# Attentions carried as side work of a projection and of two gated merges

## The reference, cut to what matters

```python
h = rms_norm(x, norm1_g)
proj = h @ w_in
y_a = mlstm_branch(...)          # ends in a norm over each head, times a gate
y_b = gqa_branch(...)            # 8 heads of 64 on 2 key heads, softmax over 512 keys
y_c = natten_branch(...)         # 8 heads of 64, windows of the 8 x 64 grid, with a bias
y_d = diff_branch(...)           # 4 heads, softmax(q1 k1) - lam * softmax(q2 k2), then a norm
g = sigmoid(gl).reshape(bsz, s, 4, D_MODEL)
merged = (g[:, :, 0] * (y_a @ w_up_a) + g[:, :, 1] * (y_b @ w_up_b)
          + g[:, :, 2] * (y_c @ w_up_c) + g[:, :, 3] * (y_d @ w_up_d))
x = x + merged @ w_out
h2 = rms_norm(x, norm2_g)
x = x + (silu(h2 @ w_ffn_gate) * (h2 @ w_ffn_up)) @ w_ffn_down
```

## Time and profile before

| what | value |
|---|---|
| median of 3 runs | 3935.73 us (3926.63 to 3938.5) |
| the profiled execution, time | 3938.49 us |
| its span from first to last instruction | 3936.6 us |
| PE busy | 3687.2 us, 94% |
| DVE, ACT, POOL busy | 2034.0 (52%), 1537.6 (39%), 399.3 (10%) us |
| mean granted PE clock, as a share of 2.4 GHz | 0.966 |

### The profile page before, as it was taken

How to read it: one execution, slowest core, us unless ns; L and a number is a source line. 1 busy time by engine, 2 the same in 40 slices (tenths; PEclk the granted TensorE clock), 3 DMA queues, 4 the chain that set the end, 5 groups by cost and what they waited for, 6 DMA issues and landing times. The chain is left out here.

```text
span 3936.6 us, 52179 instructions
## 1 busy us (share of the span) xinstructions
PE 3687.2 (94%) x20468; PEld 2879.9 (73%) x20468; DVE 2034.0 (52%) x3128; ACT 1537.6 (39%) x2410; POOL 399.3 (10%) x353
## 2 busy tenths in 40 slices
PE   7898989969999999999899999999899899999998
PEld 5456777758878887676667878887676667888887
DVE  4879565585443334646556443333546646454332
ACT  4464332543342233435453333323334444233322
POOL 0018233000011110310000001100010000001100
PEclk9899889979999999999999999999999999999999
DMA  3011001203332332120212332233111212332232
GB/s 110 22 41 59 7 2 61 70 11 117 91 100 98 97 95 85 43 70 28 97 48 88 96 100 96 96 95 92 55 59 38 82 48 81 96 102 96 96 92 80
DMA packets 83487, 289.31 MB, mean 73 GB/s; under 512 B 9168, under 2 KB 9296, under 8 KB 82000
## 3 DMA queue, kind: packets, MB, share of 16 engines
q1 hardware_dynamic: 83136, 286.30, 22.9%
q10 hardware_dynamic: 144, 0.15, 0.0%
HBM read 284.32 MB, written 2.10 MB: 73 GB/s over the span
## 5 line engine op out<-in xcount | busy, mean ns | idle before, releaser
L484 DVE TENSOR_TENSOR weights_lo_r<-raw_weights,weights_hi_r 128x1024 fp32r<-128x1024 f32 (+2 forms) x554 | 636.9, 1150 | 1457.7 <-ACT weights_hi_r L478 1457.3
L478 ACT ACTIVATE weights_hi_r<-raw_weights 128x1024 fp32r<-128x1024 f32 (+2 forms) x554 | 547.5, 988 | 1610.9 <-PE ps L553 1556.2
L552 PE MATMUL ps<-xn_r,weights_hi_r 128*128 128x512 f32 x2688 | 1056.1, 393 | 0.0
L551 PE MATMUL ps<-xn_hi,weights_hi_r 128*128 128x512 f32 x1632 | 670.1, 411 | 40.8 <-DVE weights_lo_r L484 12.1
L553 PE MATMUL ps<-xn_hi,weights_lo_r 128*128 128x512 f32 x1632 | 644.7, 395 | 0.0
L552 PEld LDWEIGHTS ps<-xn_r,weights_hi_r 128*128 128x128 f32 x2688 | 510.3, 190 | 112.8 <-issue 11.0
L551 PE MATMUL ps<-y_r,weights_hi_r 128*128 128x512 f32 x1200 | 471.8, 393 | 8.0 <-DVE weights_lo_r L484 5.9
L553 PE MATMUL ps<-y_r,weights_lo_r 128*128 128x512 f32 x1200 | 468.5, 390 | 0.0
L551 PEld LDWEIGHTS ps<-xn_hi,weights_hi_r 128*128 128x128 f32 x1632 | 312.1, 191 | 137.5 <-issue 56.8
L553 PEld LDWEIGHTS ps<-xn_hi,weights_lo_r 128*128 128x128 f32 x1632 | 311.9, 191 | 67.5
L551 PEld LDWEIGHTS ps<-y_r,weights_hi_r 128*128 128x128 f32 x1200 | 226.5, 189 | 60.3 <-issue 11.9
(11 more groups left out here) (547 smaller groups left out, 5271.5 us busy)
## 6 DMA issues: line engine op xcount, KB each, us to landing
raw_weights<-in_w_ffn_dram SPq DMA_DIRECT2D x132, 512.0 KB, 3.7
raw_weights<-in_w_down_dram SPq DMA_DIRECT2D x48, 512.0 KB, 3.5
raw_weights<-in_w_out_dram SPq DMA_DIRECT2D x24, 512.0 KB, 3.6
bias_table<-in_window_bias_dram SPq DMA_DIRECT2D x8, 1280.0 KB, 9.8
raw_weights<-in_w_down_dram SPq DMA_DIRECT2D x24, 384.0 KB, 3.1
raw_weights<-in_w_hgrn_dram SPq DMA_DIRECT2D x16, 512.0 KB, 3.5
raw_weights<-in_w_mix_ssm_dram SPq DMA_DIRECT2D x16, 512.0 KB, 3.8
raw_weights<-in_w_a_qk_dram SPq DMA_DIRECT2D x16, 512.0 KB, 3.4
```

The source lines that it names most:

```text
L478: act.activation(self.k.w_hi[:, g % 2, 0:chunk.width], self.k.raw[:, slot, 0:chunk.width], ACT.Copy)\
L484: dve.tensor_tensor(self.k.w_lo[:, g % 2, 0:chunk.width], self.k.raw[:, slot, 0:chunk.width], self.k.w_hi[:, g % 2, 0:chunk.width].bitcast ...
L551: pe.matmul(out, w_hi, x_hi, start=start, stop=False)
L552: pe.matmul(out, w_hi, x_lo, start=False, stop=False)
```

## The change

- Three attentions no longer have a stage of their own. diff runs beside the projection c (`project_beside`), gqa and after it the transposition of c's values beside a merge a (`gated_beside` with `InTurn`), window beside a merge b. The merges c and d stay in `gated_products`. The order of the merges is now a, b, c, d.
- Projection and merges beside an attention use banks 0 and 1 only, and the scores have banks 2 and 3 alone. S of step n therefore waits for the readers of step n-1, not n-2.
- In an attention piece PE does S, PV, T. A piece comes at the middle of each 24-matmul chunk as well as at the end of every chunk: 24 places in each of the three stages. gqa, diff and window have 19 pieces each on PE (16 steps and 3 to drain).
- `norm_a` runs beside the projection b, which has 6 chunks.
- The gates of these layers are made as tanh of half the logit, plus 1, times the value; the factor 1/2 goes into the split of `mixed`. The multiplication becomes a `scalar_tensor_tensor` of one instruction as before.
- The bias table of the window attention is three buffers of one pair of heads instead of one of four pairs. The fourth pair is loaded by ACT's queue.

```diff
+def project_beside(k, outputs, src, side):
...
+                for s in range(job.body):
+                    t, g = job.t0 + s, job.g0 + s
+                    if t >= 2:
+                        pe.wait_ge(tile_used, t - 1)
+                    pe.wait_ge(stream.parts_ready, g + 1)
+                    for q in range(kt):
...
+                        mm = three_passes(pe, bank(k.ps, t % 2), k.w_hi[:, g % 2, at], k.w_lo[:, g % 2, at],
+                                          src.hi[:, q, :], src.lo[:, q, :], q == 0, q == kt - 1)
+                        if q == kt // 2 - 1:
+                            next(pieces, None)
+                    mm.then_inc(stream.chunk_used, 1)
+                    next(pieces, None)
...
+def gated_beside(k, part, dst, gate, side):
...
+            for t in range(KD):
+                next(pieces, None)
+                act.wait_ge(stream.chunk_used, job.g0 + 2 * t + 1)
+                if t:
+                    act.wait_ge(summed if part.accumulate else value_taken, t)
+                open_gate(act, gate, bank(k.ps, 0), part.func).then_inc(gate_ready, 1)
+                stream.run_ahead(stream.make_hi, act, job, 0, True, 2 * t, AHEAD_PARTS)
+                next(pieces, None)
+                stream.run_ahead(stream.make_hi, act, job, 0, True, 2 * t + 1, AHEAD_PARTS)
+                next(pieces, None)
...
@@ class Attention, tensor @@
-                if n >= 2:
+                if n:
                     if self.bias_of is None:
-                        pe.wait_ge(self.exps, 2 * (n - 1))
+                        pe.wait_ge(self.exps, 2 * n)
                     else:
-                        pe.wait_ge(self.fronts, self.front * (n - 1))
+                        pe.wait_ge(self.fronts, self.front * n)
                 for s in range(2):
-                    mm = pe.matmul(bank(k.ps, 2 * (n % 2) + s), self.q_of(2 * g + s, c)[:, i * P:(i + 1) * P],
+                    mm = pe.matmul(bank(k.ps, 2 + s), self.q_of(2 * g + s, c)[:, i * P:(i + 1) * P],
...
@@ layer_branches @@
+            norm_a = HeadNorm(y_a, A_HEADS, P, f"a_norm{n}", k.const("eps")[:, 0:1], o_gate, centre=True)
+            project(k, [(f"w_b_q{n}", b_qk[:, 0:4, :], 1.0), (f"w_b_k{n}", b_qk[:, 4:5, :], 1.0),
+                        (f"w_b_v{n}", v, 1.0)], k.xn, beside=norm_a)
...
+        project_beside(k, [(f"w_c_v{n}", y_c, 1.0), (f"w_c_q{n}", c_qk[:, 0:4, :], 0.125),
+                           (f"w_c_k{n}", c_qk[:, 4:8, :], 1.0)], k.xn, diff_attention(y_d, d_qk, d_v, lam, slope))
...
+            merge_beside(k, f"w_mix_a{n}", y_a, lo_a, mixed, False, InTurn(gqa, setup))
...
+            merge_beside(k, f"w_mix_b{n}", y_b, lo_b, mixed, True, window_side)
```

More of the change, by code:

```diff
@@ L1049, in project, with open_gate, gate_product @@
         return LastTile(jobs[0].dst, *leaves, end) if leaves else None
+def open_gate(act, o, src, func):
+    return act.activation(o, src, func, scale=0.5 if func is ACT.Tanh else 1.0)
+def gate_product(dve, o, gate, value, func):
+    if func is ACT.Tanh:
+        return dve.scalar_tensor_tensor(out=o, in0=gate, scalar=1.0, in1=value, op0=ALU.add, op1=ALU.mult)
+    return dve.tensor_tensor(o, gate, value, ALU.mult)
 class Gated:
@@ new lines, with __init__, open, sync @@
+class InTurn:
+    def __init__(self, first, second):
+        self.first, self.second = first, second
+    def open(self, k, ctx):
+        self.first.open(k, ctx)
+        self.second.open(k, ctx)
+    def sync(self, sp):
+        self.first.sync(sp)
+        self.second.sync(sp)
+    def tensor(self, pe):
+        yield from self.first.tensor(pe)
+        yield from self.second.tensor(pe)
+    def scalar(self, act):
+        yield from self.first.scalar(act)
+        yield from self.second.scalar(act)
+    def vector(self, dve):
+        yield from self.first.vector(dve)
+        yield from self.second.vector(dve)
+    def gpsimd(self, pool):
+        yield from self.first.gpsimd(pool)
+        yield from self.second.gpsimd(pool)
@@ L3525, in tensor @@
                 mm.then_inc(self.pv_done, 1)
+            m = self.done(n - 2)
+            if m is not None:
+                pe.wait_ge(self.norms, self.norm * (m + 1))
+                if m:
+                    pe.wait_ge(self.taken, m)
+                for s in range(2):
+                    for j in range(NT):
+                        mm = pe.transpose(k.ps[:, 4 + s, j * P:(j + 1) * P],
+                                          self.exp[:, maps * m % self.RE, s, j * P:(j + 1) * P], k.const("ident"))
+                mm.then_inc(self.turned, 1)
             yield
@@ L3723, in scalar @@
     def scalar(self, act):
-        yield
         for m in range(4):
@@ L3759, in bias @@
         at = window_at(b) + s * w * P
-        return self.table[:, g, at:at + w * P]
+        return self.pairs[g % 3][:, at:at + w * P]
     def tensor(self, pe):
@@ L3796, in tensor @@
                 mm.then_inc(self.pv_done, 1)
+            m = n - 2
+            if 0 <= m < self.N:
+                g, b, lo, w = self.place(m)
+                pe.wait_ge(self.norms, 3 * (m + 1))
+                if m:
+                    pe.wait_ge(self.taken, m)
+                for s in range(2):
+                    for j in range(w):
+                        mm = pe.transpose(k.ps[:, 4 + s, j * P:(j + 1) * P],
+                                          self.exp[:, m % self.RE, s, j * P:(j + 1) * P], k.const("ident"))
+                mm.then_inc(self.turned, 1)
             yield
@@ L3934, in merge @@
             parts = Parts(src, lo, y_hi[:, at:at + src.shape[1], :])
-            at += src.shape[1]
-            gated.append(Gated(w, k.xn, parts, ACT.Sigmoid, bool(gated), Split(parts), 1, beside))
-        parts = Parts(mixed[:, :, :], mixed_lo[:, :, :], y_hi[:, 0:KD, :])
+            at += KD if begun else src.shape[1]
+            gated.append(Gated(w, k.xn, parts, func, bool(gated or begun), Split(parts), 1, beside))
+        parts = Parts(mixed[:, :, :], mixed_lo[:, :, :], y_hi[:, 0:KD, :], 0.5 if func is ACT.Tanh else 1.0)
         remaining = gated_products(k, gated, mixed, gate, parts)
@@ L3940, in merge, with merge_beside @@
         return project(k, [(w_out, k.x, "add")], parts, remaining, beside=Together(*sides), leaves=sides)
+def merge_beside(k, name, y, y_lo, mixed, accumulate, side):
+    with ExitStack() as ctx:
+        k.line_start(ctx)
+        y_hi = ctx.enter_context(k.nc.sbuf_tensor(f"y_hi_{k.nc.next_id()}", [P, 4, T], F32R))
+        gate = k.sbuf(ctx, "gate", [P, 1, T])
+        parts = Parts(y, y_lo, y_hi[:, :, :])
+        part = Gated(name, k.xn, parts, ACT.Tanh, accumulate, Split(parts), 1)
+        gated_beside(k, part, mixed, gate[:, 0, :], side)
 class ScaledEnd:
@@ L4166, in hybrid_program @@
+            pairs = k.sbuf(inner, "pair_bias", [P, 2, pair])
+            window_side = WindowAttention(n, y_c, c_qk, c_v, [first_pair[:, 0, :], pairs[:, 0, :], pairs[:, 1, :]])
+            merge_beside(k, f"w_mix_b{n}", y_b, lo_b, mixed, True, window_side)
+        window.close()
+        return merge(k, [(f"w_mix_c{n}", y_c, lo_c, norm_d), (f"w_mix_d{n}", y_d, lo_d, None)], f"w_out{n}",
+                     f"norm2_{n}", y_lo[:, 8:16, :], y[:, 3:6, :], ACT.Tanh, (mixed, mixed_lo))
 def hybrid_program(nc, dram, const_at, n_const, col_at, n_col):
```

308 lines of the change are left out of this document (206 added, 102 removed).

## The result

The changed kernel took 3907.71 us (median of 3, 3905.23 to 3907.77), the kernel before 3935.73 (3926.63 to 3938.5): ratio 0.9938 with a 95% interval of 0.9922 to 0.9954, 0.6% faster. The forecast was 3907. The profiled execution has a span of 3905.5 us against 3936.6.

A forecast was written before the change was run, and what follows sets the result against it. PE was taken as the bound, busy 94% of the span. Stages summed to 609.2 us a layer against 620.9 and 625.65, 28.1 gained: 3910.4 profiled, 3907 us median, range 3882 to 3934.

The forecast's parts named there:

- c with diff: Diff beside projection c: 66.3 us of projection plus 41.0 of attention, 107.3 against 126.2, gain 18.9.
- PE has the same matmuls to do, so only its pauses can be won: gqa, diff and window stages: together they hold about 27 us of PE idle time in a layer.
- The tail of `norm_a`: 10 us idle: End of projection b: PE idles 10 us behind DVE's last tiles, the stage taking 49.8 instead of 33.85 us.
- The clock behind the tail: Projection d: half clock after the new, longer pause adds 3.4 us, 88.7 becoming 92.1.
- S on one pair of banks waits for nothing: S in attention pieces: wait taken as 0, with 0.2 to 0.3 us to spare in gqa.
- The sign that I had named for the contrary: Rows of S waiting for ACT exponentials or DVE statistics: more than some 5 us a layer means waits or slower.
- The other sign: L555 behind T: a distance of 0.11 to 0.2 us, else a drain at every border.
- Second layer: Second layer's stretch: the same 609.2 us against 625.65, 16.4 gained, its extra 4.7 us put down to lower clock.
- The larger gain: Rival at `norm_a`'s tail: it holds PE less or the clock does not fall; gain 55 us, 3880; chance 0.12.
- The waits: Rival at S: gqa's reserve gone and DVE late in diff, 0.2 us at each of 96 S, 3926; chance 0.12.
- The slower case: Rival at S on single banks: late ACT or DVE stops the merge too; 3965 at 0.6 us each; chance 0.10.
- A drain at every border: Rival between projection and attention: full drain of 0.16 us at each of 114 pieces, 18 us, 3925; chance 0.06.

The follow-up runs named there:

- e4: Changed kernel with diff in a stage of its own, on two pairs of score banks, then projection c alone; 3936.66 us, ratio 1.0023 to before.
- e5: Changed kernel with gqa in a stage of its own, in its old form on two pairs of score banks; 3917.00 us, ratio 0.9961 to before.
- e1: Changed kernel with `norm_a` tighter, its pieces beside projection b moved earlier; 3882.35 us, ratio 0.9881 to before.
- e10: Changed kernel with 9 unused fp32 matmuls of constants on PE behind `norm_a`'s last one; 3900.93 us, ratio 0.9918 to before.
- e3: Changed kernel with the two layers' gates by sigmoid and a plain product instead of tanh; 3916.75 us, ratio 0.9965 to before.
- e6: Changed kernel with gqa in a stage of its own, in its new form on one pair of score banks; 4049.93 us, ratio 1.0306 to before.

## Why the prediction was right

The time, the sum and its terms held. First layer, predicted and measured: projection b 49.8 and 49.9, projection d 92.1 and 90.6, c with diff 107.3 and 109.8, merge a 120.2 and 120.5, merge b 102.7 and 103.3, merges c and d 137.1 and 137.2; in all 609.2 and 611.3.

That both layers together came out within 0.3 us (1218.4 and 1218.1) is in part luck. Projection d came out 5.7 us shorter than predicted in the two layers (184.2 and 178.5), c with diff 3.4 longer (214.6 and 218.0), the other stages 2.0 longer together. The prediction counted nothing outside the layers, where 2.7 us went by chance of the clock. And 3935.73 - 28.1 is 3907.6, where the forecast says 3907.

- *PE has the same matmuls to do, so only its pauses can be won.* Right. By part and for both layers: diff about 29 us (e4), gqa 10 (e5), window some 6 (39.46 + 66.8 - 103.3, twice; no run of its own). The `norm_a` beside projection b takes back about 18: 49.9 for 33.85 us, less the 7.0 of matmuls that leave the merges, twice. 29 + 10 + 6 - 18 = 27, of 28.4 measured; two profiles of the kernel before differ by as much (1246.6 and 1248.1).
- *The tail of `norm_a`: 10 us idle.* Right, to 0.2 us, and by its own mechanism: e1 takes VectorE's tiles forward and 8.7 us of the stage go; e10 fills PE and the stage stays.
- *The clock behind the tail.* I added 3.4 us to projection d; against before it grew by 1.9 in the first layer and by nothing in the second (88.7 and 89.0 before, 90.6 and 87.8 after). Against e10, where the pause is filled, it is 3.6 and 1.3 longer. Most of the first stretch at half clock lies in the pause itself, and in the second layer none follows the wait for `lambda`. This term was mis-sized: 6.8 us for both layers, where e10 gives 4.9.
- *c with diff* came out 2.5 us longer in the first layer, 0.9 in the second. The first layer's clock was 0.98, after a pause at the end of projection d. The rest is 0.9, at full clock (108.2 us in e1). Of it, 0.2 lies in the projection itself (66.5 alone in e4 for 66.3). Read from start to start in e1's trace, S, T and PV hold PE 38.0 us, where the prediction had 41.0, and the fp32r matmuls around them 70.3, where they take 66.5 alone. So the borders move time from the attention to the matmuls that follow a piece or precede S, and cost 0.7 to 0.8 us net, which the prediction took as 0.
- *S on one pair of banks waits for nothing.* Right; the 0.2 to 0.3 us of reserve is 0.23 by e3. The sign that I had named for the contrary, more than 5 us in the row of S waiting for the exponentials, was a bad one: 5.3 us stand there without any lost time. The starts decide, not the sum of a wait. The other sign, L555 behind T at 0.11 to 0.2 us and else a drain at every border, was bad too: L555 starts 0.03 us after the last matmul of T starts, so by its letter the sign spoke for a drain, while the distance is shorter than the range and not longer.
- *Second layer.* I took 609.2 and said that the 4.7 us more of before were clock. The second run of before (625.25 and 622.9) shows that the layers trade such stretches by chance.

The rivals. The larger gain (3880 without tail and clock loss) did not come with the change, but it was about the right price of the tail: it meant 55 us less than before, and e1, which takes the tail away, has layers 52.5 us shorter and a median 47 shorter than the kernel before in its group. The waits did not come. The slower case needed 0.3 us for each S; e6 shows PE waiting for ACT at fifteen S in the bare stage, some 2.5 us each, and that the merge's matmuls hide such waits. A drain at every border was priced at 0.16 us; the traces show 0.18 for a change behind T and 0.09 more at the entry into S (0.32 for 0.23 us). Its count was wrong: with T last, gqa and window have three changes of tile a step and diff has two, as before. The Trainium skill, TensorEngine Tiling (Array Packing), section Key Properties, says that changing the tiling mode drains the engine; the trace agrees in that a change of tile costs time, 0.18 us behind T, and the order in the piece decides how often one pays.

## What to carry to other kernels

Before side work is put beside a stage, add up what PE itself does in it by start-to-start times: only the idle part can be hidden, 29 us in two layers for diff, whose VectorE was the bound, and 10 for gqa, which was bound by PE. Then look for the engine that gets a tail at the stage's end: a norm with 3.3 us reciprocals placed two steps too late ate two fifths of what the three attentions had won. In a piece between 128\*128 matmuls put a 128\*128 group last, so that the array's tile changes once less.

## What was not expected of the hardware

- Pauses can cost more than their length. In the first layer one of 9.85 us brought half clock over 10.2 us, of which 3 lay on work, and a second stretch stood behind the next pause; the repair of both took 8.1 us from projection d, of which 3.3 us were the wait for `lambda`. In e1, where the long pause is gone, the wait for `lambda` of 2.54 us was followed by 3.4 us at half clock. In e6 fifteen waits of some 2.5 us went with a clock of 0.73 in the whole stage.
- The clock of unchanged code varies: the first block ended between 1482.7 and 1492.8 us in fourteen profiles, so single spans differ by some 10 us with nothing changed. Why it varies stays open.
- A table load between a copy and an exponential delays it by 1.42 us, with no drain of a microsecond behind it.
